# A three-block transformer on one core: gate products interleaved in PSUM, and a third buffer for gathered expert rows

## The chip, the core and the metric

The kernel runs on one core of one Trainium2 chip. The metric is the device time of one execution in microseconds (us). The core has TensorE (PE, its weight loads shown as PEld), VectorE (DVE), ScalarE (ACT), GpSimd (POOL) and SyncE (SP). The first four compute; SP, ACT and POOL also issue DMAs.

## What is computed

The input is one sequence of 512 tokens of width 1024, in float32. Two layers of a first block (feed-forward, recurrent and attention branches, feed-forward) and one layer of a second block (convolution and sparse attention, attention over a memory, and an expert layer) are followed by a final norm. The change touches only the expert layer and the way to the output:

```
def peer(hn, w_q, sub_keys, u_emb, v_emb):          # 8 heads, 128 x 128 experts, 16 chosen per head
    q = (hn @ w_q).reshape(B, T, PEER_HEADS, 2, PEER_HALF)
    s = jnp.einsum('bthpd,hpkd->bthpk', q, sub_keys)
    s_top, i_top = lax.top_k(s, 16)                  # per half
    cand = s_top[..., 0, :, None] + s_top[..., 1, None, :]
    cand_idx = i_top[..., 0, :, None] * 128 + i_top[..., 1, None, :]
    best, pos = lax.top_k(cand.reshape(...), 16)
    experts, gates = cand_idx at pos, softmax(best)
    u = u_emb[experts]                               # 128 chosen experts per token
    a = gelu(einsum('nd,nkd->nk', x, u))
    return einsum('nk,nkd->nd', gates * a, v_emb[experts])
```

Each token has 8 x 16 = 128 chosen experts of 16,384, each with a row u and a row v of 1024 numbers.

## The kernel before

Everything stands in one program for all engines, and they are held together by counting semaphores; the order on each engine is written out by hand. There is no planner. The expert layer has three stages.

**Choosing** (up to about 3684 us of the span) finds the experts and gates of every token.

**The gate matrix** (`pe_gates`, `act_gates`, `dve_gates`, `pool_gates`, lines 2679 to 2751; about 3687 to 3854 us). For the first 384 tokens ("dense" tokens), a 128 x 128 matrix per token is made: row e1, column e2 holds the gate of expert e1 * 128 + e2, or zero. It is the product of two one-hot matrices over the 128 picks of the token: OA (hot at the first index, scaled by the gate) and OB (hot at the second). A group is four tokens; there are 96 groups. For each group DVE makes the four OA and two of the OB (lines 2732 and 2735), ACT makes one OB in two instructions (HS at line 2699, OB at line 2701), POOL makes one OB in two instructions (lines 2748 and 2751), PE multiplies four times 128 x 128 x 128 in plain float32 into one PSUM bank (line 2688), and ACT copies the bank of 512 values per partition into a staging tile STG in SBUF (line 2712). Two banks and two sets of OA and OB are used in turn. PE may write the bank of group g when ACT has copied group g-2 (`gm_copied`); DVE, POOL and ACT may overwrite the hot matrices of group g-2 with those of group g when PE has finished group g-2 (`gm_full`). ACT's order per group is: hot matrix for two groups later (HS, a drain, OB), then the copy.

STG holds 64 tokens as [e2][token], so that 16 groups fill it, and then ACT issues its store to the tensor `gate_matrix` in HBM (4 MB, six times, two STG tiles in turn). Before the change, the four tokens of a group lie one after the other in the bank, [token][e2], and the copy reads the bank in order and writes each value 64 words after the one before.

**The experts** (`pe_experts`, `act_experts`, `dve_experts`, `pool_expert_loads`, lines 2764 to 2967; about 3866 to 4880 us). For the dense tokens, all 16,384 experts are computed as 128 steps of 128 experts. The steps are carried by 116 weight tiles of 1 MB, loaded into two buffers RAW by SP. 104 tiles hold u and v of one step ("single" tiles). 12 tiles ("pair" tiles, one after each eight single ones) hold the v of two steps whose first product was made in the stage before. Each tile is split into a high part WH (ACT, line 2816) and a low part WL (DVE, line 2866) in two halves, and each product is made of three float32r matmuls (lines 189 to 191). The gates of a step (GM) are loaded from `gate_matrix` by POOL, multiplied into the activations (WG, line 2877), split into WGH and WGL, and used by the second product.

For the last 128 tokens ("own" tokens), the chosen experts are gathered instead: pick n, of 128, gathers the u and v rows of one expert for each token, 1 MB, by an indirect DMA that POOL issues into a buffer UV (line 2965). `pick_dot` (DVE, line 2858) multiplies u with the token, ACT turns the sum into a coefficient (lines 2826 and 2828), `pick_sum` (DVE, line 2853) adds v times the coefficient to YG. One pick goes with each step, so a single tile has one pick, a pair tile two. DVE's order for tile x is: WL of tile x+1 first half, WG, `pick_sum` of the pick before, WGL, WL of tile x+1 second half (and WG, WGL of a pair's first step, if x+1 is a pair), `pick_dot`; in a pair tile then also `pick_dot` of the second pick and `pick_sum` of the first. UV has two buffers, so POOL waits before the gather of pick e for `pick_sum` of pick e-2 (`pick_done`), and only then comes to the loads behind it in its order. POOL's order is GM of step e (waits for WG of step e-2), gather of pick e, GM of step e+1, and so on.

At the end DVE writes the scaled output of four blocks of 128 tokens into FIN (line 2939), 16 KB per partition, and SP stores it. FIN has its own place beside UV.

Of the kernel before, what the change touches and what calls it, by code (L numbers as in the profile page):

```python
# [13 lines left out]
P = 128  # L14
# [1316 lines left out]
def allocate(c):  # L1331
    c.PB = c.stack.enter_context(c.nc.psum_tensor("PB", [P, 8, S], F32))
    c.X = c.sb("X", [P, DC, S])
    with ExitStack() as s:
        c.QZR = [[c.sb(f"QZR{v}{i}", [P, S], F32, s) for i in range(2)] for v in range(2)]
        c.QZC = [[c.sb(f"QZC{v}{i}", [P, S], F32, s) for i in range(2)] for v in range(2)]
        c.PM2, c.PT2 = c.sb("PM2", [P, 2, S], F32, s), c.sb("PT2", [P, 2, S], F32, s)
        c.OQ2, c.OB2 = c.sb("OQ2", [P, QB, P], F32, s), c.sb("OB2", [P, QB, P], F32, s)
        c.QCOS, c.QSIN = c.sb("QCOS", [P, S], F32, s), c.sb("QSIN", [P, S], F32, s)
    c.XH, c.XL = c.sb("XH", [P, DC, S], F32R), c.sb("XL", [P, DC, S], F32R)  # L1340
    c.RAW = [c.sb(f"RAW{i}", [P, TILE]) for i in range(2)]
    with ExitStack() as s:
        stage = c.sb("STG0", [P, KEYS, TOK_BLOCK], F32, s)
    c.WH = [c.sb(f"WH{i}", [P, TILE], F32R) for i in range(2)]
    c.WL = [c.sb(f"WL{i}", [P, TILE], F32R) for i in range(2)]
    c.PR = c.sb("PR", [P, LAYERS, NPRM])
    c.CT = c.sb("CT", [P, NCONST])
    c.IDENT, c.ONES, c.ONESB, c.CAUSAL, c.HMASK = (
        c.CT[:, CONSTS[n][0]:sum(CONSTS[n])] for n in ("ident", "ones", "ones_head", "causal", "head_mask"))
    c.EPSC = c.sb("EPSC", [P, 1])  # L1350
    c.SPN2 = c.sb("SPN2", [P, LAYERS, DC])
    c.SPP, c.SPN = c.sb("SPP", [P, LAYERS, DC]), c.sb("SPN", [P, LAYERS, DC])
    c.GQ8 = c.sb("GQ8", [P, LAYERS, 1])
    allocate2(c)
    c.NM, c.SUM = c.sb("NM", [P, 2]), c.sb("SUM", [P, 8])
    c.IDR, c.CAUSALR = c.sb("IDR", [P, P], F32R), c.sb("CAUSALR", [P, P], F32R)
    c.LW, c.RT = c.sb("LW", [P, 5, DC]), c.sb("RT", [P, QB])
    c.sb("ALIGN", [P, 32])


    with ExitStack() as s:
        c.SQ = c.sb("SQ", [P, DC, S], F32, s)
        c.RS = c.sb("RS", [P, S], F32, s)
    with ExitStack() as s:
        c.HH, c.HL = c.sb("HH", [P, FC, S], F32R, s), c.sb("HL", [P, FC, S], F32R, s)
        c.SIL, c.PROD = c.sb("SIL", [P, 2, S], F32, s), c.sb("PROD", [P, 2, S], F32, s)
        c.NORM_FFN = Norm(c.SQ, c.RS, c.sb("RBF", [P, S], F32, s))
    with ExitStack() as y:
        c.YH, c.YL = c.sb("YH", [P, DC, S], F32R, y), c.sb("YL", [P, DC, S], F32R, y)
        with ExitStack() as s:  # L1370
            c.ZX, c.XR, c.LG, c.AA = (c.sb(n, [P, DC, S], F32, s) for n in ("ZX", "XR", "LG", "AA"))
            c.SG = c.AA
            c.VT = c.sb("VT", [P, QB, 256], F32, s)
            c.NORM_MIX = Norm(c.SQ, c.RS, c.sb("RBX", [P, S], F32, s))
        c.M = c.sb("M", [P, DC, S], F32, y)
        with ExitStack() as s:
            c.SG2 = c.sb("SG2", [P, 4, S], F32, s)
            c.MH, c.ML = c.sb("MH", [P, DC, S], F32R, s), c.sb("ML", [P, DC, S], F32R, s)
        with ExitStack() as s:
            c.V = c.sb("V", [P, QB, D], F32, s)  # L1380
            c.CQ = c.sb("CQ", [P, S], F32, s)
            c.KZ = [c.sb(f"KZ{i}", [P, S], F32, s) for i in range(2)]
            c.QZ = [c.sb(f"QZ{i}", [P, S], F32, s) for i in range(2)]
            c.SQ2, c.RE = c.sb("SQ2", [P, 2, S], F32, s), c.sb("RE", [P, 2, QB, P], F32, s)
            with ExitStack() as f:
                c.FW = c.sb("FW", [P, 5, S], F32, f)
            c.PM, c.PT = c.sb("PM", [P, 2, S], F32, s), c.sb("PT", [P, 2, S], F32, s)
            c.OQ = c.sb("OQ", [P, QB, P], F32, s)
            c.R16, c.EXPD = c.sb("R16", [P, 16], F32, s), c.sb("EXPD", [P, 1], F32, s)
    allocate2_arena(c, stage)  # L1390


# [223 lines left out]
def allocate2_arena(c, stage):  # L1616
# [36 lines left out]
    with ExitStack() as z:  # L1653
# [29 lines left out]
        with ExitStack() as s:  # L1683

            c.AG, c.WG = c.sb("AG", [P, 2, DENSE], F32, s), c.sb("WG", [P, 2, DENSE], F32, s)
            c.WGH, c.WGL = c.sb("WGH", [P, 2, DENSE], F32R, s), c.sb("WGL", [P, 2, DENSE], F32R, s)
            c.GM = [c.sb(f"GM{i}", [P, DENSE], F32, s) for i in range(2)]
            c.UV = [c.sb(f"UV{i}", [P, 2 * D], F32, s) for i in range(2)]
            c.YG, c.PRODG = c.sb("YG", [P, D], F32, s), c.sb("PRODG", [P, D], F32, s)
            c.AV, c.CF = c.sb("AV", [P, 2], F32, s), c.sb("CF", [P, 2, 2], F32, s)  # L1690
            c.GROW = c.sb("GROW", [P, DC, P], F32, s)
            c.SQF = c.PRODG[:, :].rearrange("p (k d) -> p k d", k=DC)
            c.SS, c.RR = c.sb("SS", [P, QB], F32, s), c.sb("RR", [P, QB], F32, s)
            c.FIN = c.sb("FIN", [P, QB, D], F32, s)

# [978 lines left out]
PER_BLOCK = TOK_BLOCK // 4  # L2676


def pe_gates(c, pe, cur):
    with pe.Fori(0, GROUPS // 2) as i:  # L2680
        for j in range(2):

            pe.wait_ge(c.sem("hot_dve"), i * 2 + (j + 1))
            pe.wait_ge(c.sem("hot_act"), i * 2 + (j + 1))
            pe.wait_ge(c.sem("hot_pool"), i * 2 + (j + 1))
            pe.wait_ge(c.sem("gm_copied"), i * 2 + (j + 1))
            for q in range(4):
                last = c.nc.tensor.matmul(c.PB[:, j, q * P:q * P + P], c.OA[j][:, q, :], c.OB[j][:, q, :],
                                          start=True, stop=True)
            last.then_inc(c.sem("gm_full"), 1)  # L2690
    phase_end(c, pe, cur)


def act_gates(c, act, cur, gm):

    A = c.nc.scalar

    def hot(j, group):
        A.activation(c.HS[j][:, :], c2(c, "iota"), ACT.Square, scale=-1.0, bias=c.IT2[:, bass.ds(group * 4, 1)])
        act.drain()  # L2700
        A.activation(c.OB[j][:, 0, :], c.HS[j][:, :], ACT.Relu, scale=-1.0, bias=c.ONES[:, 0:1])\
            .then_inc(c.sem("hot_act"), 1)
    hot(0, 0)
    hot(1, 1)
    with act.Fori(0, BLOCKS // 2) as i:
        for s in range(2):
            act.wait_ge(c.sem(f"gm_stored{s}"), i * 16 + 16)
            for q in range(PER_BLOCK):

                act.wait_ge(c.sem("gm_full"), (i * 2 + s) * PER_BLOCK + (q + 3))  # L2710
                hot(q % 2, (i * 2 + s) * PER_BLOCK + (q + 2))
                c.nc.scalar.activation(c.STG[s][:, :, q * 4:q * 4 + 4].rearrange("p e t -> p t e"),  # L2712
                                       c.PB[:, q % 2, :].rearrange("p (t e) -> p t e", t=4), ACT.Copy)\
                    .then_inc(c.sem("gm_copied"), 1)
            act.drain()
            act.dma_start(gm[bass.ds(i * 2 + s, 1)].rearrange("b p e t -> (b p) e t"), c.STG[s][:, :, :])\
                .then_inc(c.sem(f"gm_stored{s}"), 16)
    act.wait_ge(c.sem("gm_stored0"), BLOCKS // 2 * 16 + 16)
    act_split(c, act, T_PEER, HEAD_P, L_EXPERTS // 2)
    phase_end(c, act, cur)  # L2720
# [126 lines left out]
def dve_experts(c, dve, cur):  # L2847
    V = c.nc.vector

    def pick_sum(n):  # L2850

        dve.wait_ge(c.sem("pick_gain"), n + 1)
        V.scalar_tensor_tensor(out=c.YG[:, :], in0=c.UV[n % 2][:, D:], scalar=c.CF[:, n % 2, 1:2], in1=c.YG[:, :],  # L2853
                               op0=ALU.mult, op1=ALU.add).then_inc(c.sem("pick_done"), 1)

    def pick_dot(n):
        dve.wait_ge(c.sem(f"rows_loaded{n % 2}"), n // 2 * 16 + 16)
        V.scalar_tensor_tensor(out=c.PRODG[:, :], in0=c.UV[n % 2][:, :D], scalar=1.0, in1=c.XG[:, :],
                               op0=ALU.mult, op1=ALU.mult, accum_out=c.AV[:, n % 2:n % 2 + 1])\
            .then_inc(c.sem("pick_dot"), 1)  # L2860

# [89 lines left out]
def pool_expert_loads(c, pool, gm, rows, gain):  # L2951
# [5 lines left out]
    for e, expert in enumerate(experts):  # L2957
        s = e % 2
        if e >= 2:
            pool.wait_ge(c.sem("wg_ready"), e - 1)  # L2960
        pool.dma_start(c.GM[s][:, :].rearrange("p (b t) -> p b t", b=BLOCKS),
                       gm[:, :, expert:expert + 1, :].rearrange("b p e t -> p b (e t)")).then_inc(c.sem(f"gm_loaded{s}"), 16)
        if e >= 2:
            pool.wait_ge(c.sem("pick_done"), e - 1)
        pool.indirect_dma_start(c.UV[s][:, :], None, rows,  # L2965
                                bass.IndirectOffsetOnAxis(ap=c.IDX[:, e:e + 1], axis=0))\
            .then_inc(c.sem(f"rows_loaded{s}"), 16)

# [295 lines left out]
```

## Time and profile before

| | us |
|---|---|
| median of 3 runs | 4902.67 |
| lowest and highest run | 4891.44, 4903.23 |
| profiled execution, its own time | 4893.58 |
| its span in the profile | 4891.6 |

The span runs from the first to the last instruction of the profiled execution; 2 us of its own time lie around it. Of the span, PE is busy 94%, DVE 57%, ACT 37%, POOL 12%, and the granted clock of TensorE is 0.967 of full speed on average. A busy share is an average over all stages; the two stages that the change touches take about 170 and 1010 us. In a row of the timeline, the first number is the start, the second the length, and the brackets at the end hold the idle time of that engine before it, and what ended it. Consecutive instructions of one kind are merged into one row (x3), and engines are pipelined, so a row can be longer than the distance to the next.

### The profile page before, as it was taken

The numbers are of one execution on the slowest core, as the hardware profiler recorded it, in microseconds if no ns is written. First come the engines' busy times: TensorE is split into PE (matmuls) and PEld (weight loads), VectorE is DVE, ScalarE is ACT, GpSimd is POOL, SyncE is SP. The second block draws the span as 40 slices with busy tenths as digits, with TensorE's granted clock in tenths as the row PEclk, the third lists the DMA queues.
The fourth block names the chain that finished last, engine by engine and source line by source line (L and its number), as shares of the span: only waits on it lengthen the run. The fifth ranks groups of instructions, "written<-read, shape, count | busy, mean of one in ns | idle before, by whom it ended". The sixth has DMA issues, their size and how long they took to land.

```text
span 4891.6 us, 62998 instructions
## 1 busy us (share of the span) xinstructions
PE 4584.9 (94%) x22315; PEld 3837.2 (78%) x22315; DVE 2774.1 (57%) x4593; ACT 1793.6 (37%) x2930; POOL 601.9 (12%) x639
## 2 busy tenths in 40 slices
PE   8999999999999999999999998997896799999998
PEld 7887787878878877877788777786665688888887
DVE  5426455454344365454543476553888766776776
ACT  3325434332232236343322323432228634343333
POOL 0000000000000000000000000000575322222221
PEclk9999999999999999999999988898999999999999
DMA  3222210222222222101222220031122577777776
GB/s 127 94 103 78 94 53 34 78 86 94 103 87 94 103 78 95 69 35 61 86 94 103 81 85 27 27 121 43 69 86 112 217 272 283 278 282 278 282 279 240
DMA packets 85649, 600.85 MB, mean 123 GB/s; under 512 B 10640, under 2 KB 11024, under 8 KB 18512
## 3 DMA queue, kind: packets, MB, share of 16 engines
q1 hardware_dynamic: 57456, 410.85, 23.0%
q0 software_dynamic: 27136, 162.28, 9.5%
q10 hardware_dynamic: 864, 25.17, 1.2%
q8 instruction: 119, 1.95, 0.2%
q14 instruction: 74, 0.61, 0.0%
HBM read 570.99 MB, written 27.26 MB: 122 GB/s over the span
## 4 chain that ended last, share of the span: by engine, by line
PE 70%; issue 14%; DVE 6%; ACT 5%; DMA 2%; DVEq 1%; ACTq 1%; POOLq 0%; POOL 0%; SPq 0%
PE PB L189 20%; PE PB L191 20%; PE PB L190 20%; PE PB L2442 3%; PE PB L896 1%; DMA UV<-rows,IDX 1%; PE PB L887 1%; ACT STG L2712 1%; PE PB L2012 1%; DVE WL L2866 1%; ACT WH L2816 1%; DVE NM L919 1%; PE PB L1092 1%; PE PB L1105 1%; ACT WH L162 1%
## 5 line engine op out<-in xcount | busy, mean ns | idle before, releaser
L189 PE MATMUL PB<-XH,WH 128*128 128x512 f32 (+1 forms) x3360 | 1294.2, 385 | 88.7 <-DVE WL L2866 30.3
L190 PE MATMUL PB<-XL,WH 128*128 128x512 f32 (+1 forms) x3360 | 1280.0, 381 | 0.0
L191 PE MATMUL PB<-XH,WL 128*128 128x512 f32 (+1 forms) x3360 | 1279.9, 381 | 0.0
L170 DVE TENSOR_TENSOR WL<-RAW,WH 128x1024 fp32r<-128x1024 f32 x520 | 642.3, 1274 | 506.5 <-ACT WH L162 487.3
L189 PEld LDWEIGHTS PB<-XH,WH 128*128 128x128 f32 x3360 | 642.8, 191 | 207.5 <-DVE WL L2866 36.5
L190 PEld LDWEIGHTS PB<-XL,WH 128*128 128x128 f32 x3360 | 642.9, 191 | 104.1 <-issue 1.5
L191 PEld LDWEIGHTS PB<-XH,WL 128*128 128x128 f32 x3360 | 641.7, 191 | 102.6
L162 ACT ACTIVATE WH<-RAW 128x1024 fp32r<-128x1024 f32 x506 | 508.3, 1050 | 557.9 <-PE PB L191 534.1
L2866 DVE TENSOR_TENSOR WL<-RAW,WH 128x1024 fp32r<-128x1024 f32 x230 | 281.9, 1226 | 244.5 <-ACT WH L2816 236.2
L248 POOL TENSOR_TENSOR SQ<-SQ 128x512 f32<-128x512 f32 x49 | 71.7, 1464 | 2354.3 <-ACT SQ L231 2343.1
L189 PE MATMUL PB<-WH,WGH 128*128 128x512 f32 x768 | 300.8, 392 | 10.2 <-DVE WGL L2881 10.2
L191 PE MATMUL PB<-WH,WGL 128*128 128x512 f32 x768 | 301.9, 393 | 0.0
L190 PE MATMUL PB<-WL,WGH 128*128 128x512 f32 x768 | 301.7, 393 | 0.0
L189 PE MATMUL PB<-HH,WH 128*128 (+1 forms) x704 | 273.9, 389 | 0.0
L190 PE MATMUL PB<-HL,WH 128*128 (+1 forms) x704 | 273.9, 389 | 0.0
L191 PE MATMUL PB<-HH,WL 128*128 (+1 forms) x704 | 273.9, 389 | 0.0
L477 DVE TENSOR_TENSOR PB<-PB,RBF 128x512 f32<-128x512 f32 x88 | 61.6, 700 | 367.3 <-PE PB L191 366.7
L2816 ACT ACTIVATE WH<-RAW 128x1024 fp32r<-128x1024 f32 x230 | 241.7, 1051 | 72.5 <-PE PB L191 70.6
L459 ACT ACTIVATE SIL<-PB 128x512 f32<-128x512 f32 x88 | 52.8, 600 | 561.5 <-DVE PB L477 561.5
L946 ACT ACTIVATE PM<-PB,NM 128x128 f32<-128x128 f32 (+3 forms) x240 | 117.9, 491 | 323.0 <-DVE NM L919 321.5
L2965 POOL DMA_INDIRECT UV<-rows,IDX x128 | 136.1, 1063 | 751.7 <-DVE YG L2853 751.1
L919 DVE TENSOR_REDUCE NM<-PB 128x1 f32<-128x128 f32 (+3 forms) x240 | 106.5, 444 | 151.6 <-PE PB L1094 73.3
(400 smaller groups left out, 7440.6 us busy)
## 6 DMA issues: line engine op xcount, KB each, us to landing
RAW<-weights SPq DMA_DIRECT2D x387, 1024.0 KB
gate_matrix<-STG ACTq DMA_DIRECT2D x6, 4096.0 KB, 11.5
GM<-gate_matrix POOLq DMA_DIRECT2D x128, 192.0 KB
X<-x SPq DMA_DIRECT2D x4, 512.0 KB, 5.5
UV<-rows,IDX POOLq DMA_INDIRECT x128, 5.7
out<-FIN SPq DMA_DIRECT2D x4, 512.0 KB, 2.6
MEMX<-mem POOLq DMA_DIRECT2D x1, 1024.0 KB, 5.1
SK<-sub_keys POOLq DMA_DIRECT2D x1, 1024.0 KB, 5.1
```

Of the source, the lines that this page charges most:

```text
L162: c.nc.scalar.activation(c.WH[p][:, cols], c.RAW[p][:, cols], ACT.Copy).then_inc(c.sem("w_hi"), 1)
L170: c.nc.vector.tensor_tensor(c.WL[p][:, cols], c.RAW[p][:, cols], c.WH[p][:, cols].bitcast(F32), ALU.subtract).then_inc(c.sem("w_split"), 1)
L189: c.nc.tensor.matmul(out, wh, xh, start=start, stop=False)
L190: c.nc.tensor.matmul(out, wh, xl, start=False, stop=False)
L191: return c.nc.tensor.matmul(out, wl, xh, start=False, stop=stop)
L248: last = c.nc.gpsimd.tensor_tensor(N.SQ[:, 0, :width], N.SQ[:, 0, :width], N.SQ[:, k, :width], ALU.add)
L919: c.nc.vector.reduce_max(c.NM[:, j % 2:j % 2 + 1], c.PB[:, 6 + j % 2, :nk], axis=AX.X, negate=True)\
L946: c.nc.scalar.activation(st.PM[:, j % 2, :nk], c.PB[:, 6 + j % 2, :nk], ACT.Exp, bias=c.NM[:, j % 2:j % 2 + 1], scale=1.0, accum_out=st.SU ...
L2442: last = c.nc.tensor.matmul(c.PB[:, 6 + half, :DENSE], U[:, k, :], c.NORM_PEER.SQ[:, k, :DENSE], start=k == 0, stop=k == DC - 1)
L2816: A.activation(c.WH[p][:, cols], c.RAW[p][:, cols], ACT.Copy).then_inc(c.sem(f"h{half}_hi"), 1)
L2866: V.tensor_tensor(c.WL[p][:, cols], c.RAW[p][:, cols], c.WH[p][:, cols].bitcast(F32), ALU.subtract)\
L2965: pool.indirect_dma_start(c.UV[s][:, :], None, rows, bass.IndirectOffsetOnAxis(ap=c.IDX[:, e:e + 1], axis=0))\
```

## The change

Three edits in the expert layer, and a place in memory:

- The four products of a group are written into the bank interleaved, [e2][token]: each matmul of 128 columns writes every fourth word of the bank (`tokens_inside`). The copy then reads the bank in order as before, and writes runs of four adjacent words, 64 words apart.
- UV has three buffers. The gather of pick e waits for `pick_sum` of pick e-3 instead of e-2. `rows_loaded` becomes three semaphores, counted accordingly.
- FIN is placed over the two RAW tiles (16 KB per partition in all), which are last read before the final stage.

```
+    with ExitStack() as s:
+        c.FIN = c.sb("FIN", [P, QB, D], F32, s)
     c.RAW = [c.sb(f"RAW{i}", [P, TILE]) for i in range(2)]
...
-            c.UV = [c.sb(f"UV{i}", [P, 2 * D], F32, s) for i in range(2)]
+            c.UV = [c.sb(f"UV{i}", [P, 2 * D], F32, s) for i in range(3)]
...
-            c.FIN = c.sb("FIN", [P, QB, D], F32, s)
...
+def tokens_inside(c, bank):
+
+    return c.PB[:, bank, :].rearrange("p (e t) -> p e t", t=4)
...
-                last = c.nc.tensor.matmul(c.PB[:, j, q * P:q * P + P], c.OA[j][:, q, :], c.OB[j][:, q, :],
+                last = c.nc.tensor.matmul(tokens_inside(c, j)[:, :, q], c.OA[j][:, q, :], c.OB[j][:, q, :],
                                           start=True, stop=True)
...
-                c.nc.scalar.activation(c.STG[s][:, :, q * 4:q * 4 + 4].rearrange("p e t -> p t e"),
-                                       c.PB[:, q % 2, :].rearrange("p (t e) -> p t e", t=4), ACT.Copy)\
+                c.nc.scalar.activation(c.STG[s][:, :, q * 4:q * 4 + 4], tokens_inside(c, q % 2), ACT.Copy)\
                     .then_inc(c.sem("gm_copied"), 1)
...
-        V.scalar_tensor_tensor(out=c.YG[:, :], in0=c.UV[n % 2][:, D:], scalar=c.CF[:, n % 2, 1:2], in1=c.YG[:, :],
+        V.scalar_tensor_tensor(out=c.YG[:, :], in0=c.UV[n % 3][:, D:], scalar=c.CF[:, n % 2, 1:2], in1=c.YG[:, :],
...
-        dve.wait_ge(c.sem(f"rows_loaded{n % 2}"), n // 2 * 16 + 16)
-        V.scalar_tensor_tensor(out=c.PRODG[:, :], in0=c.UV[n % 2][:, :D], scalar=1.0, in1=c.XG[:, :],
+        dve.wait_ge(c.sem(f"rows_loaded{n % 3}"), n // 3 * 16 + 16)
+        V.scalar_tensor_tensor(out=c.PRODG[:, :], in0=c.UV[n % 3][:, :D], scalar=1.0, in1=c.XG[:, :],
...
-        if e >= 2:
-            pool.wait_ge(c.sem("pick_done"), e - 1)
-        pool.indirect_dma_start(c.UV[s][:, :], None, rows,
+        if e >= 3:
+            pool.wait_ge(c.sem("pick_done"), e - 2)
+        pool.indirect_dma_start(c.UV[e % 3][:, :], None, rows,
                                 bass.IndirectOffsetOnAxis(ap=c.IDX[:, e:e + 1], axis=0))\
-            .then_inc(c.sem(f"rows_loaded{s}"), 16)
+            .then_inc(c.sem(f"rows_loaded{e % 3}"), 16)
```

## Rows read from the trace of the kernel before

**Rows 1.** The page, part 4: the chain that ended last, by line.
```profile
PE PB L189 20%; PE PB L191 20%; PE PB L190 20%; PE PB L2442 3%; PE PB L896 1%; DMA UV<-rows,IDX 1%; PE PB L887 1%; ACT STG L2712 1%; PE PB L2012 1%; DVE WL L2866 1%; ACT WH L2816 1%; DVE NM L919 1%; PE PB L1092 1%; PE PB L1105 1%; ACT WH L162 1%
```

**Rows 2.** Windows (stretch, length, busy time and instructions per engine, clock, DMA).
```profile
3690.00:3860.00 170.00, 113.05 (x772) 98.05 (x771) 153.13 (x569) 152.59 (x291) 95.74 (x188) 0.96 0.32 139
3880.00:4880.00 1000.00, 964.67 (x4741) 861.39 (x4739) 699.52 (x866) 395.36 (x713) 242.65 (x251) 0.99 0.77 276
```

**Rows 3.** Tile STG in the gate stage: its copies (ns min/median/max, first and last start).
```profile
L2712 ACT ACTIVATE STG<-PB x96: 1003/1034/1045, 3692.1 to 3852.7; 128x512 f32<-128x512 f32 x96
```

**Rows 4.** Timeline of one group in the gate stage, all engines, in order of time.
```profile
3754.56 1.13 PE L2688 MATMUL PB<-OB,OA 128*128 128x128 f32 x8 [0.53 <-ACT STG L2712]
3754.97 1.04 ACT L2712 ACTIVATE STG<-PB 128x512 f32<-128x512 f32 x1
3755.83 0.40 ACT L2699 ACTIVATE HS<-CT,IT 128x128 f32<-128x128 f32 x1
3755.86 0.69 DVE L2732 TENSOR_SCALAR OA<-CT,IT,GTT 128x128 f32<-128x128 f32 x2
3756.15 1.13 PE L2688 MATMUL PB<-OB,OA 128*128 128x128 f32 x8 [0.45 <-ACT STG L2712]
3756.61 1.04 ACT L2712 ACTIVATE STG<-PB 128x512 f32<-128x512 f32 x1
3757.11 1.01 DVE L2732 TENSOR_SCALAR OA<-CT,IT,GTT 128x128 f32<-128x128 f32 x3
3758.20 1.04 ACT L2712 ACTIVATE STG<-PB 128x512 f32<-128x512 f32 x1
```

**Rows 5.** Timeline of DVE in the first two groups: fourth OA of each.
```profile
3688.67 0.85 DVE L2732 TENSOR_SCALAR OA<-CT,IT,GTT 128x128 f32<-128x128 f32 x3
3690.09 0.34 DVE L2732 TENSOR_SCALAR OA<-CT,IT,GTT 128x128 f32<-128x128 f32 x1
```

**Rows 6.** A group of instructions of ACT in another stage: a contiguous copy.
```profile
L2512 ACT ACTIVATE X<-PB 128x512 f32<-128x512 f32 x8 | 4.7, 598 | 1.6 <-PE PB L2499 1.6
```

**Rows 7.** Chain of waits: 160 records of 384 columns in plain float32.
```profile
3619.82 51.62 PE PB L2442 x160
```

**Rows 8.** Timeline of PE: float32r matmuls of 384 columns, five apart.
```profile
4113.03 0.33 PE L189 MATMUL PB<-XH,WH 128*128 128x384 f32 x1
...
4113.90 0.33 PE L191 MATMUL PB<-XH,WL 128*128 128x384 f32 x1
```

**Rows 9.** Waits in the expert stage (engine and line, for whom, us, times, longest).
```profile
PE PB L189 <- DVE WL L2866: 30.3, 12, 2.8
PE PB L189 <- DVE WGL L2881: 10.2, 13, 5.9
...
ACT WH L2816 <- PE PB L191: 70.6, 82, 0.9
...
DVE PRODG L2858 <- DMA UV<-rows,IDX: 48.8, 24, 3.3
```

**Rows 10.** Timeline around the second pair tile, in order of time.
```profile
4020.87 1.07 POOL L2965 DMA_INDIRECT UV<-rows,IDX  x1 [7.99 <-DVE YG L2853]
...
4026.43 1.23 DVE L2858 SCALAR_TENSOR_TENSOR PRODG<-UV,XG 128x1024 f32<-128x1024 f32 x1 [3.04 <-DMA UV<-rows,IDX]
...
4028.17 1.04 ACT L2816 ACTIVATE WH<-RAW 128x1024 fp32r<-128x1024 f32 x1
...
4029.24 1.23 DVE L2866 TENSOR_TENSOR WL<-RAW,WH 128x1024 fp32r<-128x1024 f32 x1 [0.38 <-ACT WH L2816]
...
4030.52 0.69 PE L189 MATMUL PB<-XH,WH 128*128 128x384 f32 x1 [2.49 <-DVE WL L2866]
```

**Rows 11.** Windows of PE, 6 us from the end of a stall (busy, clock, DMA).
```profile
4030.52:4036.52 6.00, 6.00 (x26) 0.76 0.93 328
4109.78:4115.78 6.00, 6.00 (x32) 1.00 0.94 332
```

**Rows 12.** Tile UV in the expert stage: issue to landing of its gathers.
```profile
DMA to landing us min/median/max: 5.5/5.7/6.5
```

## Prediction

> **What bounds the kernel now.** I read the chain of waits first. PE's three float32r lines carry 60% of it, and two entries with a percent each belong to the change: the copy STG at L2712 and the gathers UV [rows 1]. The windows then part the two stages. In the gate stage PE is busy 113 of 170 us, but ACT 152.6 and DVE 153.1; in the expert stage PE is busy 965 of 1000 us, and no other engine is near that [rows 2]. So the first stage belongs to ACT or DVE, the second to PE, and there only PE's holes can be won.
>
> In the gate stage PE waits before each group for the copy [rows 4]. Consecutive copies start 1.64 and 1.59 us apart, a cycle of 1.61. Two things give that number. ACT alone takes it: the hot matrix begins 0.86 after the copy's start and the next copy 0.78 after that. And so does the loop PE, hot matrix on ACT, copy, PE of two groups later: PE ends at 3755.69, HS starts 0.14 later, the copy 0.78 after that, it takes 1.04, PE starts 0.14 after a copy's end (3756.01 to 3756.15) and takes 1.13; together 3.23 for two groups, 1.61 for one. Both hold the copy in full.
>
> In the expert stage PE stands still 30.3 us in 12 waits for WL, 2.5 each, and 10.2 us in 13 waits for WGL [rows 9]. There are 12 pair tiles. Around one of them the order is plain [rows 10]: POOL can issue the gather of the second pick only at 4020.87, after `pick_sum`; DVE idles 3.04 us until it lands, at 4026.43; ACT's WH and DVE's WL of the tile after next stand behind it in their orders (4028.17, 4029.24), and PE starts at 4030.52 after 2.49 us of nothing. DVE has 24 waits for UV, 48.8 us, two for each pair tile [rows 9]; the second is for the first pick behind it and shorter.
>
> **The change, part by part.**
>
> *Copy (gain).* It takes 1034 ns for 128x512 [rows 3]; the same copy with contiguous output takes 598 [rows 6]. The only difference is the hop of 64 words on writing. New: runs of four words with the same hop. Bounds: 0.60 (contiguous) and 1.03 (as now). I take 0.60, since three of four steps are now adjacent. The result hardly depends on it, as follows.
>
> With 0.60, ACT alone needs 1.61 - 0.43 = 1.18 per group, and its loop with PE (3.23 - 0.44) / 2 = 1.40. What is late next is DVE. In the first two groups it ran without waiting, and its fourth OA came 3690.09 - 3688.67 = 1.42 us apart [rows 5]: that is its own pace. Its loop with PE is a little longer, since after a wait DVE starts more slowly: 0.17 from PE's end to the first OA (3755.69 to 3755.86), 1.25 to the fourth (3757.11), 0.34 for it, about 0.10 until PE starts (0.14 is what PE needs after a copy), 1.13 for PE: 2.99 for two, 1.50 for one [rows 4, 5]. The cycle should lie between the two; I take 1.48, nearer to the loop, since 1.42 asks that DVE never waits. Any copy up to 0.76 us gives the same: the loop over ACT is then 1.48 too. Gain: 95 intervals x (1.61 - 1.48) = 12 us; 18 if DVE's 1.42 is reached, 8 if the engines jostle and it is 1.53. The 160.6 us between the first and the last copy [rows 3] are 95 x 1.61 and 8 us of pauses at the stores, which stay.
>
> *Interleaved output (cost).* No matmul of this trace writes PSUM with a step. From below: nothing, or nothing visible. What speaks for that is that plain float32 brings its columns slowly: 160 records of 384 columns took 51.62 us, 0.32 each [rows 7], where a float32r matmul of 384 columns takes 0.87 / 5 = 0.174 [rows 8]; a write has nearly two column times before the next one comes. From above: the nearest price for hopping writes is ACT's own, (1034 - 598) / 512 = 0.85 ns per value [rows 3, 6]. A group has 8 records of 128 columns, 0.84 ns a column (0.3226 / 384), 0.86 us of the 1.13; 0.85 ns more per column is 0.87 us more, PE 2.0 per group, and DVE's loop (2.99 + 0.87) / 2 = 1.93. That is 95 x 0.32 = 30 us more than now, in place of 12 fewer. Up to 2 x 1.61 - 2.99 = 0.23 us more per group (streaming a quarter slower) the stage is no slower than today. I take nothing: rows 7 and 8 are of the same operation, ACT's price is of another engine and memory. Both ends stay for the range.
>
> The Trainium skill speaks against this edit: "PSUM — Partial Sum Buffer", Specifications (TRN2), gives PSUM lines of two float32 values and says that any non-contiguous access pattern slows matmuls significantly. It has no price; by it the stage would come out as in the first rival. No row here shows such a write.
>
> *Third buffer (gain).* The gather of the second pick of a pair then waits for `pick_sum` of a pick one earlier, that is, it is issued in the tile before, some 8 us sooner; the gather needs 5.5 to 6.5 us [rows 12] and DVE missed it by 3.0. The long and the short wait both go. DVE and ACT are in order, so all behind moves up by 3.04: WH to 4025.1, WL's end from 4030.47 to 4027.4. PE was free at 4030.52 - 2.49 = 4028.03. So WL is 0.6 early here (3.04 of wait taken away, 2.49 of stall), and with stalls of at most 2.8 [rows 9] against waits of about 3 it is early in all twelve: the 30.3 us go. What is late next is PE itself. On top comes the clock: in 6 us after the stall at 4030.52 the granted clock was 0.76, half of full speed for about half of them, and 26 matmuls ran; after that at 4109.78 it was 1.00, and 32 ran [rows 11]. Of twelve such windows, one for each stall, five show 0.72 to 0.76 with 25 or 26 records, seven 1.00 with 32; one of each kind stands in the rows. Five times 6.4 of 32 records is 5 x 1.2 = 6 us. Together 36 us. The other waits remain: WGL 5.9 at the start and 12 x 0.35.
>
> The gathers themselves: POOL now passes them sooner and so reaches GM of the next step sooner, which waits for WG of its own anyway. In single tiles gathers start at the same point of the tile, only for the pick after, so they collide with the weights as now. The bytes are the same and the stage shorter, 276 GB/s become 286; 6 us with PE fully busy ran at 332 [rows 2, 11]. ACT waits for no weight load today, its waits are for PE [rows 9]. Cost: 0. If the cover is gone, see the third rival.
>
> *FIN over RAW.* No instruction more, no wait more; FIN is written after the last WL was made. 0.
>
> Sum: -12 - 36 = -48. The profiled execution took 4893.58 (span 4891.6 and 2 around it): 4846. It was 9 us under the median of the runs, 4902.67, though within their spread; the same 48 off the median is 4855. I give 4852, nearer to the median, since the runs scatter above it more than below.
>
> **Rivals.**
> 1. *The stepped output slows PE.* Place and price as above: between 0 and 30 us lost in the gate stage, the 36 kept: 4867 (stage as today) to 4897. For it: ACT's price for single-word hops [rows 3, 6]. Against: the slow columns of plain float32 [rows 7, 8]. Chance 0.20. By the rule of the Trainium skill quoted above, this rival would be the one to expect.
> 2. *The copy stays at 1.03* because runs of four don't help: cycle 1.61, only the 36 remain, 4867. Against: the copy of equal size at 0.60. Chance 0.06.
> 3. *The pair tile finds another wait*, a weight load that lands late behind the earlier gather or GM: WL comes late again and PE keeps its stall: only the 12, 4891. For it: DMA engines 0.94 busy right behind the stalls [rows 11]. Against: no wait for weights anywhere. Chance 0.09.
> 4. *Slower.* The stepped output triples the streaming time in line 2688 (a read and a write of the line for each pass, say): 0.86 x 2 = 1.72 more per group, loop (2.99 + 1.72) / 2 = 2.36, 95 x 0.75 = 71 lost, 36 won: 4938. It decides from the point where the cycle is over 1.61 + 36 / 95 = 1.99, that is 0.99 more per group, streaming 2.2 times as long. Against it: nothing in the trace writes so slowly. Chance 0.06.
>
> Both gains as forecast: 0.57, own range 4840 to 4864. The remaining 0.02 is what I don't see.
>
> **How the numbers follow.** A difference of 0.3%, 15 us, is about what a measurement of this kernel can tell from none. Under 4888 lie the forecast (0.57), most of rival 1 (0.16), rival 2 (0.06), a third of rival 3 (0.03): faster 0.82. Within 15 us: the rest of 1 and 3 and some of the unseen, 0.11. Slower: rival 4 and the rest, 0.07. The range 4836 to 4890 takes in the forecast, rival 2, most of 1 and nearly half of 3: about 0.83. Its low end is 18 + 36 off 4890, a run at the level of the lowest.
>
> **What would show it.** Copy at about 0.60 us and copies 1.42 to 1.53 apart, with PE's wait for STG gone and DVE's OA named instead. Records at line 2688 of 1.13 us per group: if they are longer, rival 1 or 4. No wait of PRODG for UV, none of PE for WL at L189, the 0.35s still there. Granted clock 1.00 through the expert stage. I am wrong if the distance from one pair tile to the next, 79.3 us between the second and the third (4030.52 to 4109.78, [rows 11]), doesn't fall to about 76, or if the gate stage doesn't shrink from 160.6 us between first and last copy to about 148.

## The result and the profile after

| | before | after |
|---|---|---|
| median of the runs (4 each, taken side by side) | 4898.26 | 4842.97 |
| lowest and highest | 4891.44, 4903.23 | 4836.49, 4849.02 |
| profiled execution | 4893.58 | 4836.49 |
| its span | 4891.6 | 4834.5 |
| mean granted clock | 0.967 | 0.970 |

The ratio is 0.9885, with a 95% interval of 0.9873 to 0.9897: 55 us faster. Predicted were a gain of 48 us and a time of 4852 us (4836 to 4890).

The two profiled executions differ by 57.1 us. Where these lie is read off by fixed points that both traces have. The first copy to STG starts at 3688.3 instead of 3692.1 [rows 3]: 3.8 us, in stages that no edit touches. From the first to the last copy it is 148.9 instead of 160.6 us: 11.7. From the last copy to PE's restart in the expert stage (3859.01, before 3874.77) 21.8 instead of 22.1: 0.3. From that restart to DVE's last addition to X (4822.19, before 4879.36) 963.2 instead of 1004.6: 41.4. The tail behind it is equal. The 3.8 are no gain: in the later profiles, of the changed kernel and of kernels that do the same up to there, the first copy started anywhere between 3685 and 3701 us.

**The gate stage.** The copies of the changed kernel, and the windows over both stages (columns as in [rows 2]); the second window ends with the stage:

```profile
L2718 ACT ACTIVATE STG<-PB x96: 574/577/580, 3688.3 to 3837.2; 128x512 f32<-128x512 f32 x96
```

```profile
3685.00:3838.00 153.00, 112.21 (x768) 94.27 (x768) 148.00 (x571) 122.61 (x288) 94.76 (x189) 0.99 0.32 137
3860.00:4820.00 960.00, 955.80 (x4743) 857.22 (x4742) 699.32 (x868) 395.76 (x714) 238.95 (x250) 1.00 0.82 289
```

The copy fell from 1034 to 577 ns, and with it ACT's busy time from 152.6 to 122.6 us, while DVE is now busy for 148 of 153. PE's waits of the gate stage, before the change (not among the rows above):

```profile
PE PB L2688 <- ACT STG L2712: 42.5, 87, 0.7
PE PB L2688 <- DVE OA L2732: 7.3, 3, 3.6
```

and after:

```profile
PE PB L2694 <- DVE OA L2737: 38.0, 87, 3.6
...
PE PB L2694 <- ACT STG L2718: 4.1, 5, 1.0
...
DVE OA L2737 <- PE PB L2694: 1.9, 3, 0.9
```

The same 87 waits are there. They are now for DVE. Two groups in the timeline of after, to be laid beside [rows 4]:

```profile
3754.72 0.40 ACT L2705 ACTIVATE HS<-CT,IT 128x128 f32<-128x128 f32 x1
3754.92 1.16 PE L2694 MATMUL PB<-OB,OA 128*128 128x128 f32 x8 [0.34 <-DVE OA L2737]
3755.49 0.58 ACT L2718 ACTIVATE STG<-PB 128x512 f32<-128x512 f32 x1
3756.03 0.93 DVE L2737 TENSOR_SCALAR OA<-CT,IT,GTT 128x128 f32<-128x128 f32 x3
3756.42 1.16 PE L2694 MATMUL PB<-OB,OA 128*128 128x128 f32 x8 [0.34 <-DVE OA L2737]
3756.99 0.58 ACT L2718 ACTIVATE STG<-PB 128x512 f32<-128x512 f32 x1
3757.54 0.93 DVE L2737 TENSOR_SCALAR OA<-CT,IT,GTT 128x128 f32<-128x128 f32 x3
```

Copies are 1.50 us apart here instead of 1.61. DVE's rows carry no bracket: it runs through without a wait. This stretch is one of the quick ones. Of the 95 distances between copies in this trace, 23 are 1.50 or 1.51, most of the others 1.53 to 1.65, and the whole stage gives 148.9 / 95 = 1.57 per group.

The pauses at the stores have changed too. Before, the copies around the second store started at 3743.06, 3746.03 and 3747.60: a pause of 2.97, then the usual distance. Now (all copies of the stretch, ACT's other rows left out):

```profile
3736.70 0.58 ACT L2718 ACTIVATE STG<-PB 128x512 f32<-128x512 f32 x1
...
3739.21 0.58 ACT L2718 ACTIVATE STG<-PB 128x512 f32<-128x512 f32 x1
...
3740.45 0.58 ACT L2718 ACTIVATE STG<-PB 128x512 f32<-128x512 f32 x1
```

A pause of 2.51, then 1.24: ACT catches up, since it has time to spare and DVE had worked on. DVE waited for PE 8.5 us in six waits before, and waits 1.9 in three now. So DVE, with hardly a wait, binds the whole stage, and its pace there is 1.57 and not 1.50.

PE's eight records take 1.16 in these rows where they took 1.13. That is not the step of four words with which every output is now written: in experiment e4 below, whose outputs are written in order, they take 1.16 as well.

```profile
3753.91 1.16 PE L2694 MATMUL PB<-OB,OA 128*128 128x128 f32 x8 [0.34 <-DVE OA L2738]
```

Nor does the group of all of them show a change (the one of before had 112.1 us and 292 ns for its 768):

```profile
L2694 PE MATMUL PB<-OB,OA 128*128 128x128 f32 x768 | 112.2, 290 | 42.4 <-DVE OA L2737 38.0 <-ACT STG L2718 4.1
```

**The expert stage.** The waits of after that answer to [rows 9]:

```profile
ACT WH L2821 <- PE PB L191: 76.1, 88, 0.9
...
PE PB L189 <- DVE WGL L2886: 11.0, 13, 6.8
...
DVE PRODG L2863 <- DMA UV<-rows,IDX: 0.2, 1, 0.2
```

PE's wait for WL, 30.3 us before, is not in the list any more, and DVE's 48.8 us for UV are 0.2. Around the second pair tile [rows 10] it now looks like this; the first row is the gather of the second pick, issued a tile earlier:

```profile
3990.28 1.06 POOL L2970 DMA_INDIRECT UV<-rows,IDX  x1 [0.34 <-DVE YG L2858]
...
4001.49 1.22 DVE L2863 SCALAR_TENSOR_TENSOR PRODG<-UV,XG 128x1024 f32<-128x1024 f32 x1
...
4002.82 1.23 DVE L2863 SCALAR_TENSOR_TENSOR PRODG<-UV,XG 128x1024 f32<-128x1024 f32 x1
...
4004.56 1.05 ACT L2821 ACTIVATE WH<-RAW 128x1024 fp32r<-128x1024 f32 x1
...
4005.64 1.23 DVE L2871 TENSOR_TENSOR WL<-RAW,WH 128x1024 fp32r<-128x1024 f32 x1 [0.39 <-ACT WH L2821]
...
4007.19 0.33 PE L189 MATMUL PB<-XH,WH 128*128 128x384 f32 x1
```

The second PRODG follows the first without a hole, WL ends at 4005.64 + 1.23 = 4006.87, and PE comes to it at 4007.19: 0.32 us in hand where PE had waited 2.49. The rows of PE at the start of the stage and at the start of two pair tiles:

```profile
3859.01 0.77 PE L189 MATMUL PB<-WH,WGH 128*128 128x512 f32 x1 [6.79 <-DVE WGL L2886]
...
3915.38 0.47 PE L189 MATMUL PB<-WH,WGH 128*128 128x512 f32 x1 [0.35 <-DVE WGL L2886]
...
3990.63 0.47 PE L189 MATMUL PB<-WH,WGH 128*128 128x512 f32 x1 [0.35 <-DVE WGL L2886]
```

Ten more like the last two follow, and nothing else stops PE. They are 75.2 us apart throughout (3990.63 - 3915.38 = 75.25).

**The clock.** Each drop can be priced by the same work with and without one. Windows of PE in the trace of before, from the end of a WL stall to just before the next pair tile, 294 matmuls each (busy, clock, DMA):

```profile
4030.52:4090.20 59.68, 59.68 (x294) 0.98 0.80 289
4109.78:4168.20 58.42, 58.42 (x294) 1.00 0.82 295
```

and single microseconds around the end of the first of these stalls, at 4030.52 (columns as in [rows 2]):

```profile
4030.00:4031.00 1.00, 0.48 (x1) 0.48 (x2) 1.00 (x3) 0.03 (x1) 1.00 (x2) 0.51 0.43 74
4031.00:4032.00 1.00, 1.00 (x5) 1.00 (x5) 1.00 (x1) 1.00 (x2) 0.01 (x1) 0.50 0.75 205
...
4033.00:4034.00 1.00, 1.00 (x6) 1.00 (x5) 0.77 (x1) 0.00 (x0) 1.00 (x2) 0.79 0.95 397
```

The clock is at 1.2 instead of 2.4 GHz from shortly after 4030.0 to 4033.4, some 3.4 us, the first half microsecond of them still in the stall. The drop costs 1.3 us here (59.68 against 58.42) and between 1.3 and 1.5 in the five of the stage: 7 us. In the changed kernel none is left there:

```profile
3915.38:4820.00 904.62, 900.77 (x4474) 1.00 0.82 288
```

How many stalls bring a drop differs from one execution to the next: in the traces of e1 and e3 below, which keep the stalls, it is two drops and three. So 7 us is the price in this execution and not a constant of the kernel.

**The 41.4, added up.** Stalls 30.3; five clock drops 7; at the start of the stage 0.5 (PE's restart to the first pair tile, 56.5 before, 56.0 after, for a reason that no run shows). The rest, about 3.5, is what a stall costs beyond its bracket. From a pair tile's start to the WL stall before, and to the same matmul after (4007.19), 78 matmuls:

```profile
3931.66:3948.40 16.74, 16.74 (x78) 1.00 0.71 253
```

```profile
3990.63:4007.19 16.56, 16.56 (x78) 1.00 0.76 265
```

The last matmul ahead of a stall runs out to its full 0.39 us where its successor would have begun 0.23 after its start (0.16 of the 0.18), and behind a stall without a drop of the clock the second matmul begins 0.28 after the first and not 0.17 (0.11). That is 0.29 for each of twelve, an estimate, since the profile models the ends of matmuls. It fits the distances: without a drop, two pair tiles were 75.5 us apart beside their stall (77.96 - 2.44 for the third and fourth), and are 75.2 now.

### The profile page after: what moved, and what is told of

It is laid out like the page before. It is cut to its first block, busy times and chain, and to the rows that moved or that the text cites. A ratio compares the mean times of both kernels' runs of the same rounds, so it can differ in the third digit from the quotient of the medians.

```text
span 4834.5 us, 62998 instructions
## 1 busy us (share of the span) xinstructions
PE 4569.3 (95%) x22315; PEld 3825.6 (79%) x22315; DVE 2769.0 (57%) x4593; ACT 1765.3 (37%) x2930; POOL 597.3 (12%) x639
## 4 chain that ended last, share of the span: by engine, by line
PE 72%; issue 15%; DVE 7%; ACT 3%; DVEq 2%; ACTq 1%; DMA 1%; POOLq 0%; POOL 0%; SPq 0%
PE PB L189 21%; PE PB L191 21%; PE PB L190 21%; PE PB L2443 3%; PE PB L896 1%; PE PB L887 1%; DVE OA L2737 1%; DVE NM L919 1%; PE PB L2013 1%; PE PB L1092 1%; DVE OB L2740 1%; PE PB L1105 1%; ACT WH L162 1%; PE PB L1114 1%; ACT WH L2821 1%
## 5 line engine op out<-in xcount | busy, mean ns | idle before, releaser
L189 PE MATMUL PB<-XH,WH 128*128 128x512 f32 (+1 forms) x3360 | 1289.9, 384 | 56.5 <-DVE XL L238 22.3
L2821 ACT ACTIVATE WH<-RAW 128x1024 fp32r<-128x1024 f32 x230 | 241.6, 1050 | 79.3 <-PE PB L191 76.1
L189 PE MATMUL PB<-YH,WH 128*128 128x512 f32 x416 | 167.4, 402 | 17.4 <-DVE WL L170 5.9
## 6 DMA issues: line engine op xcount, KB each, us to landing
gate_matrix<-STG ACTq DMA_DIRECT2D x6, 4096.0 KB, 11.7
```

The source lines that it names most:

```text
L189: c.nc.tensor.matmul(out, wh, xh, start=start, stop=False)
L2821: A.activation(c.WH[p][:, cols], c.RAW[p][:, cols], ACT.Copy).then_inc(c.sem(f"h{half}_hi"), 1)
```

## The experiments

All kernels are the changed one with the edit shown, except the first, which starts from the one before. Ratios are to the kernel before, run side by side with them (median 4899.13 beside e1 to e3, 4899.59 beside e8, 4901.10 beside e9 and e10, and one execution of 4901.04 beside e4 to e7). e4 to e7 and e10 were executed once each; from them durations in the trace are read and not differences of a few microseconds in the whole time.

**The parts alone (e1, e2), and the third buffer without its earlier issue (e3).** e1 has the interleaved bank only:

```
-                last = c.nc.tensor.matmul(c.PB[:, j, q * P:q * P + P], ...
+                last = c.nc.tensor.matmul(tokens_inside(c, j)[:, :, q], ...
-                c.nc.scalar.activation(c.STG[s][:, :, q * 4:q * 4 + 4].rearrange("p e t -> p t e"), ...
+                c.nc.scalar.activation(c.STG[s][:, :, q * 4:q * 4 + 4], tokens_inside(c, q % 2), ACT.Copy)
```

> The kernel before with the interleaved gate products alone. Theory: the two parts touch stages that follow one another and add up, so this one gives the gate stage's part only: copies 1.50 us apart as in the changed kernel, 149 us from first to last, about 12 us or 0.25% off the kernel before (ratio 0.9975), and the expert stage keeps its 12 stalls of 2.5 us for WL and the drops of the clock behind them. Rival: the two parts share something (transfers, clock), and alone it gives clearly less or more than 12.

e2 is the changed kernel with exactly these lines as they were before.

> The changed kernel with the gate products written and copied as before; the third buffer alone. Theory: no wait of PRODG for UV, no stall of PE for WL, pair tiles 75.2 us apart, 41 us or 0.85% off the kernel before (ratio 0.9915), and the gate stage at 160.6 us between first and last copy. Rival: part of the 41 us came from the gate stage (the clock at the start of the expert stage, the time at which transfers start), and it is 36 or less.

e3 has all three buffers, but the old wait:

```
-        if e >= 3:
-            pool.wait_ge(c.sem("pick_done"), e - 2)
+        if e >= 2:
+            pool.wait_ge(c.sem("pick_done"), e - 1)
```

> The changed kernel, but each gather still waits for pick_sum of the pick two earlier; three buffers, FIN over RAW and all places in memory as changed. Theory: the gain is the earlier issue alone, so the stalls come back: DVE waits 24 times for UV, about 49 us, PE 12 times for WL, about 30 us, some drops of the clock, and the time is 41 us over the changed kernel (ratio to the kernel before 0.9970 to 0.9980). Rival: buffers, places or the separate semaphores do part of it, and it stays well under the 41.

The changed kernel ran beside them:

> The changed kernel beside the others on the same chip. Theory: ratio 0.9885 to the kernel before, the sum of what the two parts give alone (0.25% and 0.85%).

| | median | ratio | first to last copy | PE for WL |
|---|---|---|---|---|
| e1, interleaving only | 4886.87 | 0.9974 (0.9963 to 0.9986) | 149.5 | 32.1 in 13 |
| e2, third buffer only | 4857.46 | 0.9917 (0.9899 to 0.9935) | 159.9 | none |
| e3, old wait | 4890.21 | 0.9983 (0.9973 to 0.9993) | 149.9 | 32.2 in 13 |
| the change again | 4845.87 | 0.9888 (0.9870 to 0.9905) | 149.7 | 0.4 in 1 |

The parts add: 0.26% and 0.83% make 1.09%, the whole shows 1.12%. About 12 us belong to the interleaving and about 42 to the buffer. e3 is as fast as e1 within the intervals, so the buffer works by nothing but the earlier issue. With the old wait both waits are back in e3:

```profile
DVE PRODG L2863 <- DMA UV<-rows,IDX: 53.7, 27, 3.6
...
PE PB L189 <- DVE WL L2871: 32.2, 13, 3.1
```

**Which side of the bank may hop (e4, e5).** In e4 PE writes each token in order, and the copy reads with a hop of 128 words and writes runs of four; in e5 PE writes pairs of tokens interleaved and the copy writes runs of two:

```
+                c.nc.scalar.activation(c.STG[s][:, :, q * 4:q * 4 + 4],
+                                       c.PB[:, q % 2, :].rearrange("p (t e) -> p e t", t=4), ACT.Copy)
```

> The changed kernel, but the products lie one after the other in the bank as before, and the copy gathers on reading: it reads the four tokens 128 words apart and writes runs of four. It moves the hop from PE's write and ACT's write to ACT's read. Theory: what cost 1.03 us was the hop of single words on writing; if a hop on reading costs the same per value, the copy is at about 1.03 again and copies are 1.61 apart; if reading PSUM with a hop is free, it is 0.58 and the cycle 1.50, and the interleaved write by PE was not needed. I expect it between, 0.7 to 1.03. Rival: any hop of single words costs ACT the same 0.85 ns a value on either side.

```
+        matmul(c.PB[:, j, (q // 2) * 256:(q // 2) * 256 + 256].rearrange("p (e t) -> p e t", t=2)[:, :, q % 2], ...
+        activation(c.STG[s][:, :, q * 4:q * 4 + 4].rearrange("p e (h t) -> p h e t", h=2),
+                   c.PB[:, q % 2, :].rearrange("p (h e t) -> p h e t", h=2, t=2), ACT.Copy)
```

> The changed kernel with the tokens interleaved by two instead of by four: PE writes every second word, the copy reads in order and writes runs of two words, 64 or 62 words apart. Theory: ACT pays for a single word per hop only, and runs of two are enough: copy 0.58 us, cycle 1.50. Rival: the price falls with the length of the run: 0.80 at runs of two; the cycle would then be 1.50 too or a little over, so the length of the copy decides, not the time.

They took 4843.05 and 4851.29 us. The copies of e4 and of e5:

```profile
L2718 ACT ACTIVATE STG<-PB x96: 575/577/580, 3692.8 to 3842.2; 128x512 f32<-128x512 f32 x96
```

```profile
L2718 ACT ACTIVATE STG<-PB x96: 577/600/606, 3701.1 to 3850.6; 128x512 f32<-128x512 f32 x96
```

Reading PSUM value by value across 128 words costs ACT nothing (577 ns), where 0.7 to 1.03 us were expected. It is the write into SBUF that must not hop at every value; runs of two words suffice. Their 600 ns are no price of the shorter run: in e8 below, copies with runs of four take 597. So e4's order of the copy's loops alone brings the whole gain of the stage (149.4 us between first and last copy), and PE's stepped write was not needed. The Trainium skill, "SBUF — State Buffer", Specifications (TRN2), says that full rate needs at least two hits per line of 16 bytes; by that two adjacent float32 values are enough, and the 600 ns of e5 against 1034 agree.

**What a stepped write costs PE (e6, e7).** e6 adds matmuls at the end of PE's program, into a free bank, first in order and then with a step:

```
+    for _ in range(40):
+        T.matmul(B, W16, M16, start=True, stop=True)                                      # L2818
+    for _ in range(40):
+        T.matmul(B.rearrange("p (e t) -> p t e", t=2), W16, M16, start=True, stop=True)   # L2820
+    for _ in range(40):
+        T.matmul(B.rearrange("p (e t) -> p t e", t=4), W16, M16, start=True, stop=True)   # L2822
+    for _ in range(40):
+        T.matmul(B.rearrange("p (e t u) -> p t e u", t=2, u=2), W16, M16, ...)            # L2824
... the same with float32 operands, in order (L2826) and with a step of four (L2828), and further groups
```

> The changed kernel with matmuls added at PE's end, each kind by its own line, all into a bank that nothing reads: bfloat16 128x512 with output in order, with steps of 2 and 4 words, in runs of two words with a hop, plain float32 128x512 in order and with step 4, 128 columns in order and with step 4. Theory: plain float32 brings a column every 0.84 ns, half the pace of a one-pass matmul, and hides what a stepped write costs: both float32 pairs are equal; bfloat16 with a step is slower than in order, up to twice, and runs of two are as fast as in order. Rival A: no stepped write costs anything in any type. Rival B: float32 is slower too with a step, and the gate stage only hid it behind DVE.

Its groups on PE (busy us, mean ns):

```profile
L2822 PE MATMUL PB<-CT 128*128 128x512 bf16 x40 | 17.4, 634 | 0.0
L2820 PE MATMUL PB<-CT 128*128 128x512 bf16 x40 | 17.3, 633 | 0.0
L2828 PE MATMUL PB<-AE,CT 128*128 128x512 f32 x40 | 17.3, 592 | 0.0
L2826 PE MATMUL PB<-AE,CT 128*128 128x512 f32 x40 | 17.3, 592 | 0.0
...
L2824 PE MATMUL PB<-CT 128*128 128x512 bf16 x40 | 8.8, 380 | 0.0
L2818 PE MATMUL PB<-CT 128*128 128x512 bf16 x40 | 8.8, 379 | 0.0
```

A bf16 matmul of 512 columns takes 8.8 / 40 = 0.22 us in order and with runs of two words, and 0.43 with single words two or four apart. In plain float32 each of 20 matmuls leaves two records of 0.43, in order or not. In the shape of the gate stage, 128 columns of plain float32, 80 records took 9.1 us in order and 9.1 with a step of four. (The whole kernel took 4952.21, the added work included.)

e7 asks the same of accumulating writes, in the 384-column products of the choosing stage, whose bank is then read back by ACT with the same step:

```
-                last = c.nc.tensor.matmul(c.PB[:, 6 + half, :DENSE], U[:, k, :]
+                last = c.nc.tensor.matmul(c.PB[:, 6 + half, :].rearrange("p (e t) -> p t e", t=4)[:, :3, :], U[:, k, :]
```

> The changed kernel with the output of the early products (L2443 of the changed kernel, plain float32, 384 columns, accumulated over eight) also written with step 4 and read by ACT with step 4. These products are bound by PE: 32 records take 10.32 us. Theory: accumulation makes no difference, 10.3 us stay. Rival: a stepped output that adds to what is in the bank reads and writes a line for each word, and the 10.3 become 12 to 20 us.

It took 4848.75, and the row that answers to [rows 7] is the same to the last digit:

```profile
3626.05 51.62 PE PB L2443 x160
```

**What sets the pace of the gate stage (e8, e9, e10).** e8 gives the gate stage four sets of hot matrices and four banks, so that DVE may run further ahead of PE:

```
-        c.OA = [c.sb(f"OA{i}", [P, 4, P], F32, q) for i in range(2)]
+        c.OA = [c.sb(f"GOA{i}", [P, 4, P], F32, q) for i in range(4)]
... the same for OB, HS and HP; the loops over groups step by four; gm_full and gm_copied start at 4
```

> The changed kernel with four sets of hot matrices and four banks in turn in the gate stage, so that DVE waits for the product four groups back instead of two, and ACT makes its hot matrix before it waits for the product it copies. Theory: the cycle of 1.50 is the loop of DVE and PE over two groups (0.17 + 1.59 + 0.1 + 1.16, halved); with four sets DVE runs at its own pace of 1.42, 95 x 0.08 = 8 us less than the changed kernel (0.16%). Rival: 1.50 is DVE's own pace in a loop (the branch, the registers for the token numbers, POOL beside it), and nothing is won.

The changed kernel ran beside it a third time:

> The changed kernel on the same chip as the one with four sets, for the comparison: ratio 0.9885 to the kernel before; the one with four sets 0.9869 by the theory, 0.9885 by the rival.

4842.4, ratio 0.9883 (0.9867 to 0.9900), against 4844.56, 0.9889 (0.9872 to 0.9905): the same. First to last copy 149.2 against 148.5. DVE no longer waits for PE at all, and its triples of OA still start 1.60 and then 1.57 apart:

```profile
3754.41 0.97 DVE L2738 TENSOR_SCALAR GOA<-CT,IT,GTT 128x128 f32<-128x128 f32 x3
...
3756.01 0.97 DVE L2738 TENSOR_SCALAR GOA<-CT,IT,GTT 128x128 f32<-128x128 f32 x3
```

The loop between DVE and PE is not the bound. Without a wait for PE, DVE takes 149.2 / 95 = 1.57 per group, which is what the changed kernel takes too.

e9 spares DVE an instruction per group, making two of the hot matrices OB at once:

```
-                if q in (1, 2):
-                    V.tensor_scalar(c.OB[j][:, q, :], iota, c.IT2[:, bass.ds(tok, 1)], None, ALU.is_equal)
+                if q == 1:
+                    V.tensor_tensor(c.OB[j][:, 1:3, :], iota.unsqueeze(1).to_broadcast([P, 2, P]),
+                                    c.IT2[:, bass.ds(tok, 2)].unsqueeze(2).to_broadcast([P, 2, P]), ALU.is_equal)
```

> The changed kernel with DVE's two one-hot matrices OB of a group made by one instruction of 128x256 instead of two of 128x128. Theory: after the change the gate stage is bound by DVE's own instructions, so every 0.1 us less of them per group shortens it by 9 us. Two OB take 0.26 + 0.20 from start to start today; one of 256 values should take about 0.35, so the cycle falls from 1.50 to 1.39 to 1.42, where the loop over ACT and PE (1.40) takes over: 8 to 10 us, ratio 0.9868 to the kernel before. Rival: the stage is bound by a loop with PE or by something beside DVE; then DVE only waits more and the ratio stays 0.9888.

4845.99, ratio 0.9880 (0.9860 to 0.9900): the interval holds both expectations, but the trace decides. First to last copy is 149.8 us, no gain. Two single instructions hold DVE for 0.20 and 0.19 us, counted from the start of each to the start of what follows; the merged one, counted so, for 0.34 to 0.43. It saves 0.05 at most and often nothing, so e9 doesn't show what a shorter DVE would bring.

e10 leaves POOL's OB out after the first two groups: HP is not made, and the second instruction covers two columns and writes no OB. The gates of every fourth token are wrong in this kernel.

```
-            G.tensor_scalar(c.OB[j][:, 3, :], c.HP[j][:, :], 0.0, None, ALU.is_equal).then_inc(c.sem("hot_pool"), 1)
+            G.tensor_scalar(c.HP[j][:, 0:2], c.HP[j][:, 0:2], 0.0, None, ALU.is_equal).then_inc(c.sem("hot_pool"), 1)
```

> The changed kernel in which POOL makes its hot matrix only for the first two groups (for all later ones it leaves it out and runs one instruction of two columns; the gates of every fourth token are wrong then). Theory: DVE's 1.42 in the first groups and 1.50 later differ because POOL's instructions beside it slow DVE; without them the cycle is 1.42. Rival: POOL has nothing to do with it, and the cycle stays 1.50.

It took 4834.97, and 140.9 us from the first to the last copy, 8.0 less. DVE's two groups of instructions in the gate stage, in the changed kernel and then in e10 (busy us, mean ns):

```profile
L2737 DVE TENSOR_SCALAR OA<-CT,IT,GTT 128x128 f32<-128x128 f32 x384 | 124.8, 362 | 11.2 <-ACTq L120 9.1 <-PE PB L2694 1.9
L2740 DVE TENSOR_SCALAR OB<-CT,IT 128x128 f32<-128x128 f32 x192 | 55.9, 291 | 0.0
```

```profile
L2737 DVE TENSOR_SCALAR OA<-CT,IT,GTT 128x128 f32<-128x128 f32 x384 | 117.8, 343 | 13.4 <-ACTq L120 9.1 <-PE PB L2694 4.2
L2740 DVE TENSOR_SCALAR OB<-CT,IT 128x128 f32<-128x128 f32 x192 | 53.7, 280 | 0.0
```

The means fall because single instructions do. Here is an OA of the changed kernel that started while POOL made its HP, with POOL's row, and the same OA of a group in e10:

```profile
3756.36 0.52 POOL L2753 TENSOR_TENSOR HP<-CT,IT 128x128 f32<-128x128 f32 x1 [0.30 <-PE PB L2694]
...
3756.55 0.42 DVE L2737 TENSOR_SCALAR OA<-CT,IT,GTT 128x128 f32<-128x128 f32 x1
```

```profile
3756.33 0.34 DVE L2737 TENSOR_SCALAR OA<-CT,IT,GTT 128x128 f32<-128x128 f32 x1
```

The median OA is no shorter with POOL at rest (342 ns, against 335 in the changed kernel). Copies in e10 are 1.42 and 1.47 apart in turn, and DVE waits for PE again at the stores (4.2 us in all, in six waits), which is why the stage shrank by 8.0 us and not by more. So DVE's pace is 1.42 with POOL at rest, as in the first two groups, and 1.50 to 1.65, 1.57 on average, beside POOL's work. Through which port or lock POOL delays DVE, no run here shows, nor why some stretches run at 1.50.

## Why the prediction was right

- **What binds each stage**: right. The copy stood in both of the gate stage's limits, and WL behind the gather was PE's only large wait in the expert stage.
- **The copy**, 0.60: measured 0.577. That any copy up to 0.76 would give the same was not tried.
- **The cycle**, 1.48, with pauses of 8 us at the stores on top: 95 x 1.48 + 8 = 148.6 us from the first to the last copy. Measured 148.9, and 11.7 us of gain where 12 were forecast. The number held by luck. Measured is 1.57 per group with the pauses in it: the cycle was forecast too short by 95 x 0.09 = 8.5 us, and the pauses, "which stay", are no longer felt, since DVE works through them and ACT catches up. The two errors cancel. The step that failed in the cycle is the reading of [rows 5] as DVE's pace in the loop: those are the first two groups, where POOL had done its own part early and then waited 2 us. In the steady loop POOL works beside DVE and stretches it (e10), and more buffers, the cure that the forecast's loop calls for, bring nothing (e8).
- **The interleaved output at nothing**: right, and for the reason given as far as the runs reach. Single-word steps double a bf16 matmul, which brings its columns at twice the rate of plain float32, and leave plain float32 alone, accumulating or not (e6, e7). Rivals 1 and 4 are out, and with the copy at 0.577 so is rival 2. The rule of the Trainium skill quoted in the prediction ("PSUM — Partial Sum Buffer", Specifications (TRN2)) is true of the bf16 matmul, at a factor of two, and not of this kernel's; nor is it true of every non-contiguous pattern, since runs of two words were free. The 8-byte line that it names fits both.
- **The third buffer**, stalls of 30.3: all gone, and e3 shows that the earlier issue did it. WL is early by 0.32 at the second pair tile, where 0.6 was forecast; most of the difference is that PE comes 0.16 sooner, as it need not run its last matmul out. Rival 3 is out.
- **The clock**, 6: the five drops were there and went, at 7. The term that was missing is 0.29 for each stall beside its bracket, 3.5 in all, and 0.5 at the start. That makes 41.4 in place of 36, and with 11.7 from the gate stage and 3.8 of scatter upstream the 57.1 in place of 48.
- **What stays**: the waits for WGL are 12 x 0.35 as forecast; the first grew from 5.9 to 6.8, while the time from the last copy to PE's restart stayed at 22 us. FIN over RAW cost nothing that shows.
- **The distance of pair tiles**, forecast to fall from 79.3 to about 76: 75.25.
- **4852 against 4843**: off by 9. The medians lie 55 us apart and not 48 (5 of these 7 are the expert stage, the rest is within the scatter), and the forecast started from 4900 where the median of before is 4898.26.

## What to carry to other kernels

If a copy hops on its way into SBUF, put the hop on the PSUM side of it and write runs of at least two words: that is an edit of one instruction. When PE stalls once per tile, follow the late operand back through the in-order queues until something waits for a buffer; a buffer there is worth the stall, 0.3 us for the broken pipeline and, at some of the stalls, a clock drop of 1.4. Read an engine's own pace in the steady loop, with its neighbours at work, and over the whole stage: neither the first rounds (1.42) nor one quick stretch (1.50) was the 1.57 that counts.

## What the runs showed of the hardware

- A write of single words two or four apart into PSUM doubles a bf16 matmul of 512 columns (0.22 to 0.43 us) and costs a plain float32 one nothing (0.43 per record); runs of two words cost nothing.
- ACT copies 128x512 float32 from PSUM in 577 to 600 ns when it writes runs of four or of two, and in 1034 word by word, 64 words apart. Reading PSUM word by word across 128 words is free.
- POOL's work beside DVE makes DVE's comparisons of 128x128 longer on average, from 343 to 362 and from 280 to 291 ns; the one that starts beside POOL's HP takes 0.42 us in place of 0.34. DVE's pace goes from 1.42 to 1.57 us per group.
- Of twelve like stalls of 2.4 to 2.8 us, five brought some 3.4 us at 1.2 GHz and seven did not; the length does not tell the two kinds apart (2.49 to 2.58 and 2.39 to 2.78).
